# Feed-forward products as three products of two-part float32r operands, with the weights split on ScalarE and VectorE and the inner chunks in three groups

## The reference, cut to what matters

```
def rmsnorm(x, w):
    y = x32 * lax.rsqrt(jnp.mean(x32 * x32, axis=-1, keepdims=True) + EPS)
    return (y * w).astype(x.dtype)

def swiglu(x, w_gate, w_up, w_down):          # 1024 -> 2816 -> 1024
    return (jax.nn.silu(x @ w_gate) * (x @ w_up)) @ w_down

h = h + concat([o_gdn, o_fox]) @ w_out[l]     # output projection
h = h + swiglu(rmsnorm(h, ffn_norm_w[l]), w_gate[l], w_up[l], w_down[l])
h = rmsnorm(h, final_norm_w)                  # then the second block
```

## Time and profile before

| | |
|---|---|
| timed runs | 2535.07, 2536.41, 2539.01 us, median 2536.41 us |
| profiled execution | first to last instruction (span) 2538.5 us; no other time of this execution is given |
| busy over the span | PE 2501.5 us, PEld 1379.5, DVE 1310.1, ACT 788.0, POOL 1045.9 |
| output projection | 503.78 to 531.53 us |
| feed-forward, gate and up | 531.53 to 836.95 us |
| feed-forward, down | 836.95 to 988.63 us |
| expert layer, `up` part | from 1366 to 2028 us |

### The profile page before, as it was taken

How to read it: one execution, slowest core, us unless ns; L and a number is a source line. 1 busy time by engine, 2 the same in 40 slices (tenths; PEclk the granted TensorE clock), 3 DMA queues, 4 the chain that set the end, 5 groups by cost and what they waited for, 6 DMA issues and landing times.

```text
span 2538.5 us, 32426 instructions
## 1 busy us (share of the span) xinstructions
PE 2501.5 (99%) x10971; PEld 1379.5 (54%) x11035; DVE 1310.1 (52%) x2691; ACT 788.0 (31%) x1287; POOL 1045.9 (41%) x727
## 2 busy tenths in 40 slices
PE   8999999999999999999999999999999999999999
PEld 6887777644444445544554444444444455555555
DVE  4422455343432202643595898222222289888888
ACT  3312223210000002222313555445444433333332
POOL 0001111010000010000188888888888366578884
PEclk9999899999999999999999999999999999999999
DMA  6330100244344222294244666666666799999997
GB/s 198 67 69 9 42 14 10 76 161 161 132 163 158 68 68 73 67 357 144 80 83 80 150 155 154 150 150 154 155 149 150 218 364 386 367 358 362 367 364 285
DMA packets 420830, 426.42 MB, mean 168 GB/s; under 512 B 104328, under 2 KB 336904, under 8 KB 420624
## 3 DMA queue, kind: packets, MB, share of 16 engines
q1 hardware_dynamic: 342928, 358.01, 43.3%
q0 software_dynamic: 77824, 67.41, 12.2%
HBM read 364.28 MB, written 61.05 MB: 168 GB/s over the span
## 4 chain that ended last, share of the span: by engine, by line
PE 97%; DVE 2%; ACT 1%; issue 0%; SPq 0%; DMA 0%; POOL 0%; DVEq 0%; ACTq 0%; POOLq 0%
PE psum L1173 11%; PE psum L1438 9%; PE psum L1437 9%; PE psum L1436 8%; PE psum L1460 7%; PE psum L1461 7%; PE psum L1459 6%; PE psum L1197 6%; PE psum L1211 6%; PE psum L850 5%; PE psum L1417 4%; PE psum L1065 1%; PE psum L1042 1%; PE psum L1023 1%; PE psum L1052 1%; PE psum L930 1%
## 5 line engine op out<-in xcount | busy, mean ns | idle before, releaser
L747 POOL DMA_INDIRECT dense_gates<-arena x384 | 607.6, 1582 | 151.7 <-issue 116.7
L1438 PE MATMUL psum<-arena 128*128 128x512 bf16 x1023 | 387.7, 379 | 1.6
L1437 PE MATMUL psum<-arena 128*128 128x512 bf16 x993 | 376.3, 379 | 1.7
L1436 PE MATMUL psum<-arena 128*128 128x512 bf16 x992 | 376.0, 379 | 0.1
L1460 PE MATMUL psum<-arena 128*128 128x384 bf16 x1024 | 335.9, 328 | 0.0
L1461 PE MATMUL psum<-arena 128*128 128x384 bf16 x1024 | 334.8, 327 | 0.0
L2437 DVE TENSOR_TENSOR arena<-arena,psum 128x1024 bf16<-128x1024 f32 x124 | 151.4, 1221 | 349.2 <-ACT psum L1789 348.5
L1459 PE MATMUL psum<-arena 128*128 128x384 bf16 x1024 | 330.8, 323 | 0.0
L727 POOL TENSOR_TENSOR arena<-arena 128x512 f32<-128x512 f32 x25 | 31.5, 1270 | 699.5 <-ACT arena L1693 428.0
L1173 PE MATMUL psum<-arena 128*128 128x512 f32 x672 | 288.9, 592 | 1.1 <-DVE arena L1895 1.1
L1805 ACT ACTIVATE arena<-arena 128x1024 bf16<-128x1024 f32 x128 | 135.3, 1057 | 303.6 <-PE psum L1461 278.6
(11 more groups left out here) (356 smaller groups left out, 3412.5 us busy)
## 6 DMA issues: line engine op xcount, KB each, us to landing
arena<-in_uT SPq DMA_DIRECT2D x128, 512.0 KB, 4.5
arena<-in_v SPq DMA_DIRECT2D x128, 512.0 KB, 5.3
gelu_spill<-cst SPq DMA_DIRECT2D x128, 256.0 KB, 3.4
arena<-in_ada_w SPq DMA_DIRECT2D x12, 2048.0 KB, 13.4
dense_gates<-arena SPq DMA_DIRECT2D x4, 6144.0 KB, 39.9
arena<-gelu_spill SPq DMA_DIRECT2D x128, 192.0 KB, 5.4
arena<-dense_gates SPq DMA_DIRECT2D x128, 192.0 KB, 7.1
arena<-in_w_in SPq DMA_DIRECT2D x20, 1024.0 KB, 7.3
```

Source lines behind the costliest of these rows:

```text
L747: pool.indirect_dma_start(gate_cells, bass.IndirectOffsetOnAxis(ap=cell_of[:, n:n + 1], axis=0), gate_of[:, n:n + 1], None, compute_op=ALU ...
L1436: mm(psum[:, bank, :], hi[:, c, :], h2hi[:, c, :], start=c == 0, stop=False)
L1437: mm(psum[:, bank, :], hi[:, c, :], h2lo[:, c, :], start=False, stop=False)
L1438: last = mm(psum[:, bank, :], lo[:, c, :], h2hi[:, c, :], start=False, stop=c == DC - 1)
```

## The change: what it does

Every feed-forward operand is held as a high part, rounded to float32r by writing it so, and a low part, the float32r of the rest. Each product becomes three: hi by hi, hi by lo, lo by hi, added in PSUM. The work is cut into 68 units (UNITS) of one weight block each: 22 gate and 22 up blocks of 128x1024, and 8 down blocks for each of three groups of inner chunks (0 to 7, 8 to 15, 16 to 21; the last group's are 128x768). The order is: gate and up of a group, then its down products, which are added to the activations; then the next group. SP loads units into a ring of 4, ACT and DVE split them into rings of 3. The root-mean-square factor is no longer put on the activations: DVE multiplies the gate product by it, and POOL multiplies silu by it for the up side, so `uT`, `xw` and `first_tile` go. `mod_tile` is cut in two halves (`mod_step`), placed behind the gate part of k 0 to 19 and behind down units 1 and 5 of the first two groups. Some semaphores are shared, buffers move, and the second block's first weights (`F_Q2`, `F_KV2`) wait for `mod_acc` instead of `out_done`. The core of the diff:

```diff
+GROUPS = ((0, 8), (8, 16), (16, 22))
+UNITS = 2 * FC + DC * len(GROUPS)
+RAW, SPLIT = 4, 3
...
     # SP
+            def load_unit(u):
+                if u >= RAW:
+                    sp.wait_ge(S["unit_lo"], u - RAW + 1)
...
+                sp.dma_start(raw[u % RAW][:, 0:n].rearrange("p (c n) -> p c n", n=P), src).then_inc(S[f"load{u % RAW}"], 16)
...
+            for u in range(RAW):
+                load_unit(u)
             for k in range(2):
+                sp.wait_ge(S["out_done"], 4 * k + 4)
                 load_ada(k)
...
+            for u in range(RAW, UNITS):
+                load_unit(u)
+                for k in range(2, MOD_TILES):
+                    if u == mod_done[k - 2] + 5:
+                        load_ada(k)
...
     # POOL
+            for k in range(FC):
+                pool.wait_ge(S["ffn_sil"], k + 1)
+                pool.tensor_tensor(sil[:, k % 2, :], sil[:, k % 2, :], rstd[:, 0, 0:SEC], ALU.mult).then_inc(S["ffn_root"], 1)
...
     # PE
+            def product3(out, u, c, x_hi, x_lo, start, stop):
+                w_hi, w_lo = (w[u % SPLIT][:, c * P:(c + 1) * P] for w in (wh, wl))
+                mm(out, w_hi, x_hi, start=start, stop=False)
+                mm(out, w_hi, x_lo, start=False, stop=False)
+                return mm(out, w_lo, x_hi, start=False, stop=stop)
+
+            def gate_up_unit(k, g):
+                u = gate_unit(k) + g
+                pe.wait_ge(S["unit_lo"], u + 1)
+                if k >= 2:
+                    pe.wait_ge(S["ffn_hid" if g else "ffn_gate"], k - 1)
...
+            def down_product(p, f):
+                u, (lo, hi) = down_unit(p, f), GROUPS[p]
+                pe.wait_ge(S["unit_lo"], u + 1)
+                pe.wait_ge(S["res_done"], DC * (p + 1) + f - 1)
...
     # ACT
+            def unit_high(u):
+                act.wait_ge(S[f"load{u % RAW}"], LOADED[u % RAW] + 16 * (u // RAW + 1))
+                if u >= SPLIT:
+                    act.wait_ge(S["unit_done"], u - SPLIT + 1)
+                n = unit_width(u)
+                f_(wh[u % SPLIT][:, 0:n], raw[u % RAW][:, 0:n], ACT.Copy).then_inc(S["unit_hi"], 1)
...
+                    u = gate_unit(k)
+                    unit_high(u + SPLIT)
+                    act.wait_ge(S["ffn_gate"], k + 1)
+                    f_(sil[:, k % 2, :], sil[:, k % 2, :], ACT.Silu).then_inc(S["ffn_sil"], 1)
+                    unit_high(u + 1 + SPLIT)
+                    act.wait_ge(S["ffn_hid"], k + 1)
...
+                    f_(hh[k - lo][:, :], tmp[:, k % 2, :], ACT.Copy).then_inc(S["part_hi"], 1)
...
     # DVE
+            def unit_low(u):
+                dve.wait_ge(S["unit_hi"], u + 1)
+                n = unit_width(u)
+                dve.tensor_tensor(wl[u % SPLIT][:, 0:n], raw[u % RAW][:, 0:n], wh[u % SPLIT][:, 0:n].bitcast(F32),
+                                  ALU.subtract).then_inc(S["unit_lo"], 1)
...
+                    dve.wait_ge(S["unit_done"], u + 1)
+                    dve.tensor_tensor(sil[:, k % 2, :], psum[:, k % 2, :], rstd[:, 0, 0:SEC], ALU.mult).then_inc(S["ffn_gate"], 1)
+                    unit_low(u + SPLIT)
+                    if u in MOD_AT:
+                        mod_step(MOD_AT[u])
+                    dve.wait_ge(S["unit_done"], u + 2)
+                    dve.wait_ge(S["ffn_root"], k + 1)
+                    dve.tensor_tensor(tmp[:, k % 2, :], sil[:, k % 2, :], psum[:, 2 + k % 2, :], ALU.mult).then_inc(S["ffn_hid"], 1)
+                    unit_low(u + 1 + SPLIT)
+                    dve.wait_ge(S["part_hi"], DC + k + 1)
+                    dve.tensor_tensor(hl[k - lo][:, :], tmp[:, k % 2, :], hh[k - lo][:, :].bitcast(F32), ALU.subtract
+                                      ).then_inc(S["part_lo"], 1)
+                for f in range(DC):
+                    u = down_unit(p, f)
+                    residual(f, "unit_done", u + 1)
+                    if u + SPLIT < UNITS:
+                        unit_low(u + SPLIT)
+                    if u in MOD_AT:
+                        mod_step(MOD_AT[u])
+                    if p == 0 and f == 2:
+                        parts = angles()
+                        table(sinT, 0.0)
+                    elif p == 0 and f == 6:
+                        table(cosT, 0.25)
```

More of the change, by code:

```diff
@@ L14 @@
 BF16 = mybir.dt.bfloat16
+F32R = mybir.dt.float32r
 I32 = mybir.dt.int32
@@ L557, in _ @@
[L557 to L569, removed]
+            for u in range(RAW, UNITS):
[3 more added lines that the diff above has]
+                        load_ada(k)
+                if u == 8:
+                    sp.dma_start(posi.bitcast(I32), io["positions"].rearrange("(o t) -> o t", o=1).to_broadcast([P, SEC])).then_inc(S["table_in"], 16)
@@ L1167, in gate_up_tile @@
[L1167 to L1174, removed]
-                last.then_inc(S["ffn_ps"], 1)
-            for n in range(FC // 2):
-                w = slot[(F_GU + n) % 2].rearrange("p (g c n) -> p g c n", g=2, c=DC)
-                pe.wait_ge(*fill_done(F_GU + n))
-                for k in range(2):
-                    if n == 0 and k == 0:
-                        first_tile(w)
-                        pe.wait_ge(S["std_ready"], 3)
-                        pe.wait_ge(S["u_ready"], 3 * DC)
-                    else:
-                        gate_up_tile(w, k, 2 * n + k - 1 if n else None)
@@ new lines, in _ @@
+            for p, (lo, hi) in enumerate(GROUPS):
+                for k in range(lo, hi):
+                    gate_up_unit(k, 0)
+                    if k == 0:
+                        mean_sum(sqf, SUMS)
+                        mean_last(1, sqf)
+                    gate_up_unit(k, 1)
+                for f in range(DC):
+                    down_product(p, f)
+                    if p == 2 and f == 1:
+                        pe.wait_ge(S["mod_acc"], MOD_TILES + 1)
+                        mm(psum[:, 7, 0:MODS * P // Q], fold, modq, start=True, stop=True).then_inc(S["mod_sum"], 1)
@@ L2145, in _ @@
-            normed(1, SEC, xT2, col_fn)
-            dve.wait_ge(S["ffn_ps"], 1)
-            dve.tensor_tensor(sil[:, 0, :], psum[:, 0, :], rstd[:, 0, 0:SEC], ALU.mult).then_inc(S["u_ready"], 1)
-            def mod_tile(k):
-                dve.wait_ge(S[f"ada_in{k % 2}"], 16 * (k // 2 + 1))
-                out = macc[:, k * MOD_W:(k + 1) * MOD_W]
-                settle(dve.tensor_scalar(out, ada[k % 2][:, 0, :], cact[:, 0:1], None, ALU.mult))
-                for c in range(1, DC):
-                    ins = stt(out, ada[k % 2][:, c, :], cact[:, c:c + 1], out, ALU.mult, ALU.add)
+                residual(f, "out_done", f + 1)
@@ new lines, in _, with mod_step @@
+                if f:
+                    x_low(f - 1)
+                if 4 <= f < 4 + SPLIT:
+                    unit_low(f - 4)
+            x_low(DC - 1)
+            dve.wait_ge(S["std_ready"], 3)
+            settle(dve.reciprocal(rstd[:, 0, 0:SEC], rstd[:, 0, 0:SEC]))
+            def mod_step(n):
+                k, half = divmod(n, 2)
+                if not half:
+                    dve.wait_ge(S[f"ada_in{k % 2}"], 16 * (k // 2 + 1))
+                    settle(dve.tensor_scalar(macc, ada[k % 2][:, 0, :], cact[:, 0:1], None, ALU.mult))
+                for c in range(4 * half if half else 1, 4 * half + 4):
+                    ins = stt(macc, ada[k % 2][:, c, :], cact[:, c:c + 1], macc, ALU.mult, ALU.add)
@@ L2155, in mod_tile @@
                     if c < DC - 1:
                         settle(ins)
+                if not half:
+                    return
                 ins.then_inc(S["mod_acc"], 1)
                 dve.wait_ge(S["mod_acc"], k + 1)
-                settle(dve.transpose(turned, out))
+                settle(dve.transpose(turned, macc))
                 settle(dve.tensor_reduce(modq[:, k * MOD_W // Q:(k + 1) * MOD_W // Q],
```

283 lines of the change are left out of this document (155 added, 128 removed).

## The result

The changed kernel took 2440.95 us (median of 4 runs, 2435.41 to 2441.99) against 2537.71 for the kernel before: ratio 0.9616, 95% interval 0.9599 to 0.9632. Timed again beside the last experiments it came to 2432.14 us and 0.9586 (0.9572 to 0.9599); why two series differ by 9 us is told at the end. Forecast: 2425, range 2414 to 2480. The direction and the mechanism (one stream for each float32r product, and a weight load that hides) were right, and the gain was overestimated: 111.5 us in the profiled execution, of which 100.2 came. The median lies above the 2420 to 2436 us that the prediction gave to its own case, in the part of the range that it kept for a split that paces the units; that case did not come, as the profile shows.

A forecast was written before the change was run, and what follows sets the result against it. PE bounds the kernel, busy 99% of the span. The feed-forward falls from 457.10 to 345.6 us (341.5 matmuls, 2.1 means and small product, 2 waits), so 2538.5 - 111.5 = 2427.0 profiled, 2425 us median; range 2414 to 2480.

The forecast's parts named there:

- its own case: Whole run: one stream per float32r product, loads hidden, few new waits; median 2425 us, 2420 to 2436, chance 0.77.
- a split that paces the units: Rival, feed-forward: DVE's chain or queued loads overrun by 1 to 3 us per k; 2445 to 2485 us, chance 0.11.
- One float32r stream per product: Feed-forward matmuls on PE: each float32r matmul takes 0.2156 us, the bfloat16 pace; 1584 of them take 341.5 us.
- two streams: Rival, feed-forward matmuls: each float32r matmul needs two streams, 0.4299 us; 2764 us, slower, chance 0.06.
- exposed loads: Rival, feed-forward matmuls: the weight load does not hide and adds 0.192 us each; 2728 us, slower, chance 0.03.
- four streams: Rival, feed-forward matmuls: float32r runs as float32, 0.860 us per matmul; 3445 us, chance 0.01.
- New waits, 2 us: Feed-forward stage: handovers between engines cost PE 0 to 9.5 us of issue gaps, taken as 2 us.
- check of the turn to a down group: First down product: newest hidden chunk ready after about 3 us; PE needs it after 4.5 us, 3.2 in the last group.
- DVE 247 us, 8.9 to 9.4 for each k: DVE in the feed-forward: busy 247 of 346 us, and 8.9 to 9.4 of 10.35 us per inner chunk.
- POOL's multiply at 1.27 us: Between Silu and the up product: POOL takes 1.27 us, done 2.6 us after the gate, before the up unit ends.
- What follows the feed-forward is as before: Stages behind the feed-forward: PE stays full there, their time is unchanged, and nothing gives the gain back.
- DMA: Feed-forward loads: weight units at share 0.40 plus `ada` tiles at 0.30, together 0.70; landings fit.

The follow-up runs named there:

- e7: Changed kernel with every 512-column matmul done as two of 256 columns over the same weights; gate and up matmuls then started 0.1200 us apart.
- e4: Changed kernel with high and low parts stored as bfloat16 in the same places, less exact; feed-forward stage 345.72 us, run 2415.57 us, ratio 0.9515.
- e1: Kernel before with only the two lines rounding buffer bases base0 and base2 up to 8 floats; 2529.63 us against 2538.67, ratio 0.9965.
- e9: Changed kernel with the hidden activations' parts moved to start at a multiple of 256 bytes; 2435.05 us, ratio 0.9596 against the kernel before.
- e10: The changed kernel itself, unedited, timed again against the same runs of the kernel before; 2432.14 us, ratio 0.9586.

## Why the prediction was right or wrong

- *One float32r stream per product* ("I take 0.2156"): the reading was right, one stream and a hidden load, and two streams, exposed loads and four streams are refuted. The size was off: 0.2267 and 0.2343 us. The step that failed is the choice of the bfloat16 row for the pace to the last nanosecond; the nearest four-byte rows would not have given the 11 ns either, since a float32 record pays 3. The sum: 363.1 us of matmuls instead of 341.5. By e7 the first 11 ns are a price for each matmul, which a count of streams could not show.
- *New waits, 2 us:* PE idled 0.2 us in the stage by the table (365.70 of 365.91), next to nothing, because the dearer matmuls gave DVE more time. At the price that was forecast (e4) 2.1 us came. The size was right, but not the place: the prediction's own check of the turn to a down group found room to spare, and that is where PE waited.
- *DVE 247 us, 8.9 to 9.4 for each k:* 254.7 us, which is near by luck (below), and at the end of a group 10.4 us for one k, from 615.70 to 626.07. The chain of the changed kernel at the first turn (start, us, what):

```profile
615.75 1.07 ACT unit_hi L1716
616.85 1.23 DVE unit_lo L2228
618.07 1.71 DVE arena L2249
619.80 0.76 DVE arena L2249
...
623.64 0.69 DVE arena L2300
624.32 1.14 DVE unit_lo L2228
625.46 0.61 DVE hid_lo L2303
626.12 0.50 PE psum L1220
```

  The first multiply-add takes 1.71 us of the chain and not 0.76. It starts while POOL's new multiply still runs; POOL's row, then all multiply-adds and all first multiplies of a `mod_tile` (ns, min/median/max):

```profile
617.41 1.80 POOL L793 TENSOR_TENSOR arena<-arena 128x512 f32<-128x512 f32 x1 [9.07 <-ACT arena L1731]
...
L2249 DVE SCALAR_TENSOR_TENSOR arena<-arena x84: 745/752/1782, 546.9 to 842.7; 128x512 f32<-128x512 f32 x84
L2247 DVE TENSOR_SCALAR arena<-arena x12: 480/1515/1523, 545.4 to 828.4; 128x512 f32<-128x512 f32 x12
```

  I priced DVE's work as if alone, and POOL's multiply at 1.27 us (measured 1.54 to 1.81). The 10 multiply-adds and 10 multiplies that began beside POOL took about 1.78 and 1.515 us, the others 0.752 and 0.480: 20.6 us of the 254.7. Without these waits DVE would have been busy for 234 us, 13 under the forecast, so two errors cancel. The rival "the split paces the units" came closer than its 0.11 says: PE lost about 1 us at the three turns, by the starts of its matmuls.
- *"What follows the feed-forward is as before":* wrong by 9.6 us, in the change's favour. The two alignment lines were in the diff, and the prediction did not price them; e1 shows them in 7.6 us, the second stage and the down part, and leaves the 1.7 us of the first to scatter. So the profiled execution came out 11 us above its forecast and not 20: +20.3 in the stage, -9.6 behind it, +0.7 ahead of it. That two misses partly cancelled is luck; the median is 16 us above its forecast.
- *DMA:* PE never waited for a load, as forecast; the share was 0.51 over the stage, where 0.70 was put for a stretch with `ada` tiles.

## What to carry to other kernels

A three-product float32r scheme gave 457 to 366 us in the matmul stage, and the split of 128x1024 weights on ACT and DVE hid behind units of 24 matmuls. Price a float32r matmul from its own stream, not from bfloat16, and with 512 columns place its moving operand a multiple of 256 bytes from its weights: 3.6 us of this stage. Read every line of a diff that moves a buffer: bases at 12 modulo 16 bytes cost untouched stages 7.6 us, and e1, two lines, was the cheapest gain of the study. Before a gain outside the changed stage is explained, look how much the same stage differs between kernels that are alike there.

## What the runs showed that I had not expected

Two things beside the prices above. First, DVE and POOL hold each other up. In all 20 cases above POOL's multiply had begun, DVE's next instruction was a multiply or multiply-add, and that one ended 0.3 to 0.55 us after POOL's. The subtraction that DVE was in when POOL began kept its 1.22 us, so not every DVE instruction suffers: the one that starts second does. The Trainium skill's page "SBUF — State Buffer" (section "SBUF: two separate sides") tells of a port pair of DVE and POOL that one of them holds for its whole instruction while the other waits; these rows agree.

Second, why whole runs scatter by 10 us. The mean granted clock of a run goes with its time: at 0.990 the changed kernel took 2440.07 to 2441.99 us, at 0.994 2430.72 and 2430.77. Stretch 262 to 380 us, long before the change, where small matmuls alternate with waits: the granted clock differs between executions of one program. Kernel e9, then e10:

```profile
262.00:380.00 118.00, 114.01 (x786) 88.80 (x786) 63.04 (x223) 33.15 (x99) 25.55 (x24) 0.93 0.09 30
```
```profile
262.00:380.00 118.00, 114.02 (x705) 87.84 (x704) 56.63 (x202) 30.29 (x91) 24.07 (x22) 0.83 0.09 30
```

At a mean of 0.93 PE gets through 786 records, at 0.83 (more of the stretch at 1.2 GHz) through 705, and the output projection's second half starts at 495.59 or at 506.43 us. These stretches have PE idle for short times between the matmuls; what decides for one or the other is open. The first stage behind the feed-forward does the same on a smaller scale, 183.73 to 186.68 us at 1.00 to 0.98. It hides gains of a few us in the run's time, so the stage is the place to read them.
